# A two-layer decoder trunk on Trainium2: another order of loads, pooling and sums in the first stage

## What is computed

```python
h = rms_norm(x, norm_g[i, 0]) * (1.0 + scale1) + shift1
y = pool_mixer(h)      # layer 0;  layer 1: differential attention
x = x + gate1 * rms_norm(y, norm_g[i, 1])
h = rms_norm(x, norm_g[i, 2]) * (1.0 + scale2) + shift2
y = swiglu(h)          # layer 0;  layer 1: top-2-of-8 experts
x = x + gate2 * rms_norm(y, norm_g[i, 3])
```

## Time and profile before

| | |
|---|---|
| median of three runs | 1278.63 us |
| the profiled execution's own time | 1280.07 us |
| its span | 1278.2 us |
| TensorE busy | 1249.0 us, 98% |
| VectorE, ScalarE, GpSimd busy | 387.3, 214.7, 109.8 us |
| mean granted TensorE clock | 0.991 of full speed |
| moved by DMA | 477.47 MB, mean 374 GB/s |
| first FFN matmul (end of the first stage) | 70.39 us |

### The profile page before, as it was taken

One profiled execution on the slowest core, in us unless ns is written; L12 is line 12 of the kernel. 1 busy time (PEld: TensorE's weight loads), 2 busy tenths in 40 slices (PEclk: granted clock), 3 DMA queues, 4 the chain that ended last, 5 costly groups with the idle time before them and its releaser, 6 DMA issues.

```text
span 1278.2 us, 31266 instructions
## 1 busy us (share of the span) xinstructions
PE 1249.0 (98%) x14625; PEld 779.1 (61%) x14625; DVE 387.3 (30%) x591; ACT 214.7 (17%) x320; POOL 109.8 (9%) x134
## 2 busy tenths in 40 slices
PE   6799999999999999999999999999999999999997
PEld 3589999989774354545455454554545545454555
DVE  1567778979872110101101011010101201011012
ACT  3253333474842000000000000000000000000001
POOL 4220000010030000020010010002001000200100
PEclk9899999999999999999999999999999999999999
DMA  9998998959379999999999999999999999999980
GB/s 371 414 358 295 334 333 305 364 197 395 123 245 420 425 423 425 424 402 424 424 407 424 424 409 411 424 409 404 423 421 396 422 424 412 404 424 415 399 355 36
DMA packets 114055, 477.47 MB, mean 374 GB/s; under 512 B 10944, under 2 KB 37280, under 8 KB 113792
## 3 DMA queue, kind: packets, MB, share of 16 engines
q1 hardware_dynamic: 106112, 457.29, 89.1%
q0 software_dynamic: 7664, 17.87, 4.6%
q10 hardware_dynamic: 144, 0.26, 0.1%
HBM read 465.79 MB, written 11.16 MB: 373 GB/s over the span
## 4 chain that ended last, share of the span: by engine, by line
PE 95%; DVE 2%; ACT 1%; POOL 1%; DMA 1%; issue 1%; SPq 0%; DVEq 0%; ACTq 0%
PE ps L2421 23%; PE ps L2407 23%; PE ps L2396 23%; PE ps L1927 7%; PE ps L1928 7%; PE ps L1929 7%; PE ps L1952 1%; PE ps L2014 1%; PE ps L1911 1%; DMA raw<-w_mod 1%; DVE wlo L1572 1%; PE ps L2205 1%; PE ps L1975 0%; PE ps L2035 0%; PE ps L2350 0%
## 5 line engine op out<-in xcount | busy, mean ns | idle before, releaser
L1799 DVE TENSOR_TENSOR act_in<-act_in,ps 128x1344 f32<-128x1344 f32 x16 | 24.9, 1555 | 527.1 <-PE ps L2407 527.1
L1927 PE MATMUL ps<-thi,whi 128*128 128x256 f32 x480 | 136.0, 283 | 0.8 <-DVE wlo L1421 0.8
L1928 PE MATMUL ps<-tlo,whi 128*128 128x256 f32 x480 | 135.8, 283 | 0.0
L1929 PE MATMUL ps<-thi,wlo 128*128 128x256 f32 x480 | 135.8, 283 | 0.0
L2396 PE MATMUL ps<-raw,turned_in 128*32 128x448 f32 x1296 | 123.7, 539 | 0.0
L2407 PE MATMUL ps<-ring_w,turned_in 128*32 128x448 f32 x1248 | 120.6, 539 | 0.0
L2421 PE MATMUL ps<-ring_w,turned_act 128*32 128x256 f32 x2016 | 117.2, 379 | 0.0
L2421 PE MATMUL ps<-raw,turned_act 128*32 128x256 f32 x2016 | 115.5, 379 | 0.0
L1220 ACT ACTIVATE act_in<-ps 128x1344 f32<-128x1344 f32 x16 | 20.7, 1292 | 548.6 <-PE ps L2396 548.6
L1290 DVE TENSOR_TENSOR wlo<-raw,whi 128x2048 fp32r<-128x2048 f32 x41 | 92.9, 2289 | 32.7 <-ACT whi L901 32.7
L2421 PEld LDWEIGHTS ps<-raw,turned_act 128*32 128x32 f32 x2016 | 82.4, 110 | 33.5 <-issue 3.5
(11 more groups left out here) (324 smaller groups left out, 1332.0 us busy)
## 6 DMA issues: line engine op xcount, KB each, us to landing
raw<-moe_w_gu SPq DMA_DIRECT2D x96, 896.0 KB, 12.9
ring_w<-moe_w_gu SPq DMA_DIRECT2D x96, 896.0 KB, 13.0
raw<-w_mod SPq DMA_DIRECT2D x84, 512.0 KB, 5.7
rows<-moe_w_gu SPq DMA_DIRECT2D x48, 896.0 KB
raw<-moe_w_down SPq DMA_DIRECT2D x48, 896.0 KB, 13.9
ring_w<-moe_w_down SPq DMA_DIRECT2D x48, 896.0 KB, 13.4
raw<-ffn_w_gu SPq DMA_DIRECT2D x44, 512.0 KB, 5.6
rows<-moe_w_down SPq DMA_DIRECT2D x24, 896.0 KB
```

Source lines behind the costliest of these rows:

```text
L1799: dve.tensor_tensor(act_3, act_3, gate_up_ps(1), ALU.mult).then_inc(e_act, 1)
L1927: pe.matmul(out, a_hi, b_hi, start=start, stop=False, skip_group_check=check)
L1928: pe.matmul(out, a_hi, b_lo, start=False, stop=False, skip_group_check=check)
L1929: return pe.matmul(out, a_lo, b_hi, start=False, stop=stop, skip_group_check=check)
```

## The change

Nothing is computed in another way; transfers, matmuls and copies are put in another order, with other banks.

- **Loads.** The tokens are loaded first, ahead of unit 0; the bands follow unit 0. A unit's load now waits until the unit two before it has landed (units 2 to 11).
- **TensorE.** After unit 1 it pools; unit 2, `spread` 1 (banks 2 and 3), unit 3 and the turn of group 1 come behind the pooling, then `m1`, unit 4, and the mix of tile 1. Units 5, 7 and 9 follow that mix. Group 4's columns are turned ahead of the first token turn. Units are called one at a time, in the same order.
- **ScalarE.** The squares of the tokens come first, then the copies of columns and distances, the scalings, and both wide copies ahead of group 1's sum.
- **Banks.** Groups 1 and 3 in bank 1, 0 and 4 in bank 0; `m1` in bank 1, gate1's sum in banks 2 and 3, `keep_clock` in bank 3.
- **Zeros** are written by VectorE at its start, and TensorE waits for them once, at its start.

```diff
@@ -49,7 +49,7 @@
 HEAD_ORDER = (1, 0, 4, 3)
 HEAD = [(1, 0), (1, 1), (1, 2), (1, 3), (0, 0), (0, 1), (2, 0), (0, 2), (2, 1), (0, 3), (2, 2), (2, 3),
         (4, 0), (4, 1), (4, 2), (4, 3), (3, 0), (3, 1), (3, 2), (3, 3)]
-HEAD_BANK = {1: 7, 0: 0, 4: 2, 3: 3}
+HEAD_BANK = {1: 1, 0: 0, 4: 0, 3: 1}
 WIDE = 6
@@ -123,7 +123,7 @@
 ROW_ORDER = [[2, 5], [3, 2, 4, 5]]
-ROW_BANK = [[None, None, 0, None, None, 2], [None, None, 0, 2, 6, 6]]
+ROW_BANK = [[None, None, 2, None, None, 2], [None, None, 0, 2, 6, 6]]
 ROW_GAIN = {2: 1, 4: 2, 5: 3}
@@ -556,8 +556,8 @@
         def _(sp):
             def load(r, rounds, halves):
-                if 3 <= r < RAW + WIDE:
-                    _, landed, n = head_slot(r - 3)
+                if 2 <= r < RAW + WIDE:
+                    _, landed, n = head_slot(r - 2)
                     sp.wait_ge(landed, n)
                 if RAW + WIDE <= r < R_FFN + RAW:
                     u = r - RAW - WIDE if r < 2 * RAW + WIDE else r - RAW
@@ -604,11 +604,11 @@
             sp.dma_start(silu_c[:, :], c.rearrange("a (p k) -> (a p) k", k=KC)).then_inc(c_loaded, 16)
+            sp.dma_start(xs[:, :, :], x[0].rearrange("(t p) d -> p t d", p=P)).then_inc(x_loaded, 16)
             for r, (g, pair) in enumerate(HEAD):
                 load(r, 0, mod_unit(0, g, pair))
-                if r == 1:
+                if r == 0:
                     sp.dma_start(pool_band, pool_in.rearrange("p (g s) -> p g s", g=4)).then_inc(pool_loaded[0], 16)
-                    sp.dma_start(xs[:, :, :], x[0].rearrange("(t p) d -> p t d", p=P)).then_inc(x_loaded, 16)
                 if r == 3:
                     sp.dma_start(poolw, pool_w[0].rearrange("g (c p) e -> p g c e", p=P)).then_inc(pool_loaded[1], 16)
@@ -728,7 +728,6 @@
             pool.memset(bias_row[:, S:S + P], NEG).then_inc(dist_ready, 1)
             pool.memset(minus_half[:, :], -0.5).then_inc(half_ready, 1)
             pool.memset(rows[:, 5, :], 0.0).then_inc(rows_zeroed, 1)
-            pool.memset(zeros[:, :], 0.0).then_inc(zeros_ready, 1)
             pool.wait_ge(rows_zeroed, 2)
             pool.dma_start(rows[0:1, 5, :], b_mod[0:1, 5 * D:6 * D]).then_inc(bmod_loaded[1], 16)
@@ -934,22 +933,20 @@
             act.wait_ge(c_loaded, 16)
             act.activation(silu_c[:, :], silu_c[:, :], ACT.Silu).then_inc(silu_ready, 1)
+            def copy_wide(i, b, dst):
+                act.wait_ge(wide_ps, i + 1)
+                act.copy(dst.rearrange("p (h d) -> p h d", h=2), ps[:, b:b + 2, :]).then_inc(wide_ready, 1)
+            for t in range(T):
+                square_x(0, t)
             act.wait_ge(cols_ps, 1)
...
             act.activation(bias_row[:, 0:S], ps[0:NH, 5, 0:S], ACT.Copy, scale=HD ** 0.5).then_inc(dist_ready, 1)
-            def copy_wide(i, b, dst):
-                act.wait_ge(wide_ps, i + 1)
-                act.copy(dst.rearrange("p (h d) -> p h d", h=2), ps[:, b:b + 2, :]).then_inc(wide_ready, 1)
-            for t in range(T):
-                square_x(0, t)
-            copy_wide(0, 2, rows[:, 6, :])
             for t in range(T):
                 normalize_tile(0, t)
+            copy_wide(0, 2, rows[:, 6, :])
+            copy_wide(1, 2, gain[:, 1, :])
             head_sum(1)
             act.wait_ge(col_ready, 1)
             for b in range(4):
@@ -957,7 +954,6 @@
                 for k in (2 * b, 2 * b + 1):
                     act.activation(pooled_t[:, k, :], ps[:, 4 + b, (k % 2) * S:(k % 2) * S + S], ACT.Copy,
                                    scale=modc[:, 0, k:k + 1]).then_inc(pooled_ready, 1)
-            copy_wide(1, 1, gain[:, 1, :])
             square_mixed(1)
             head_sum(0)
             square_mixed(0)
@@ -1378,6 +1374,7 @@
                 dve.wait_ge(col_step, i + 1)
                 return dve.tensor_tensor(modc[:, 2 * i, :], modc[:, 4, :], cols[:, 6 + i, :], ALU.mult)
+            dve.memset(zeros[:, :], 0.0).then_inc(zeros_ready, 1)
             dve.wait_ge(pool_loaded[0], 16)
             dve.tensor_copy(pool_m[:, :, 0:EDGE], pool_band[:, :, BAND:BAND + EDGE]).then_inc(pool_placed, 1)
             dve.tensor_copy(pool_m[:, :, EDGE:P], pool_band[:, :, EDGE:P]).then_inc(pool_placed, 1)
@@ -1394,7 +1391,7 @@
                 dve.wait_ge(pooled_ready, k + 1)
                 g = k // 2
-                dve.scalar_tensor_tensor(pooled_t[:, k, 0:EDGE], ps[:, 3, g * EDGE:g * EDGE + EDGE], modc[:, 1, k:k + 1],
+                dve.scalar_tensor_tensor(pooled_t[:, k, 0:EDGE], ps[:, 1, g * EDGE:g * EDGE + EDGE], modc[:, 1, k:k + 1],
                                          pooled_t[:, k, 0:EDGE], ALU.mult, ALU.add).then_inc(pooled_done, 1)
             gate_unit(2)
             gate_unit(3)
@@ -1962,35 +1959,14 @@
                                    start=True, stop=True, skip_group_check=True)
                 mm.then_inc(col_ps, 1)
-            pe.wait_ge(silu_ready, 1)
-            head_units(range(0, 2))
-            pe.wait_ge(consts_loaded, 16)
-            pe.wait_ge(mcol_loaded, 64)
-            pe.transpose(ps[:, 6, 0:9 * KC], mcol, ident[0:9 * KC, 0:9 * KC]).then_inc(cols_ps, 1)
-            pe.wait_ge(small_loaded, 32)
-            pe.matmul(ps[0:NH, 5, 0:S], relb, onehot, start=True, stop=True).then_inc(dist_ps, 1)
             def spread(i, b):
...
                 mm.then_inc(wide_ps, 1)
-            pe.wait_ge(scale_loaded, 16)
-            spread(0, 2)
-            head_units(range(2, 4))
-            turn_columns(1)
-            pe.wait_ge(wide_ready, 1)
-            pe.wait_ge(pool_placed, 2)
-            for g in range(4):
-                mm = pe.matmul(ps[:, 3, g * EDGE:g * EDGE + EDGE], ones, pool_band[:, g, 0:EDGE], start=(g == 0), stop=True,
-                               skip_group_check=True)
-            mm.then_inc(m1_ps, 1)
-            pe.wait_ge(dist_ready, 2)
-            pe.wait_ge(col_ready, 1)
-            pe.wait_ge(h_ready, T)
-            for b in range(4):
+            def pooled(b):
                 for t in range(T):
                     for k in (2 * b, 2 * b + 1):
                         c0 = (k % 2) * S
@@ -2003,10 +1979,6 @@
                                            start=False, stop=True, skip_group_check=True)
                 mm.then_inc(pooled_ps, 1)
-            pe.wait_ge(first_gain_loaded, 16)
-            spread(1, 1)
-            head_units((4, 5))
             def mix(t):
                 for g in range(4):
@@ -2016,14 +1988,45 @@
                                        start=(g % 2 == 0 and k == 0), stop=(k == 1), skip_group_check=True)
                 mm.then_inc(mix_ps, 1)
+            pe.wait_ge(zeros_ready, 1)
+            pe.wait_ge(silu_ready, 1)
+            head_units((0,))
+            pe.wait_ge(consts_loaded, 16)
+            pe.wait_ge(mcol_loaded, 64)
+            pe.transpose(ps[:, 6, 0:9 * KC], mcol, ident[0:9 * KC, 0:9 * KC]).then_inc(cols_ps, 1)
+            pe.wait_ge(small_loaded, 32)
+            pe.matmul(ps[0:NH, 5, 0:S], relb, onehot, start=True, stop=True).then_inc(dist_ps, 1)
+            pe.wait_ge(scale_loaded, 16)
+            spread(0, 2)
+            head_units((1,))
+            pe.wait_ge(pool_placed, 2)
+            pe.wait_ge(h_ready, T)
+            pe.wait_ge(cols_ready, 1)
+            pe.wait_ge(dist_ready, 2)
+            for b in range(4):
+                pooled(b)
+            head_units((2,))
+            pe.wait_ge(wide_ready, 1)
+            pe.wait_ge(first_gain_loaded, 16)
+            spread(1, 2)
+            head_units((3,))
+            turn_columns(1)
+            pe.wait_ge(wide_ready, 2)
+            pe.wait_ge(col_ready, 1)
+            for g in range(4):
+                mm = pe.matmul(ps[:, 1, g * EDGE:g * EDGE + EDGE], ones, pool_band[:, g, 0:EDGE], start=(g == 0), stop=True,
+                               skip_group_check=True)
+            mm.then_inc(m1_ps, 1)
+            head_units((4,))
+            pe.wait_ge(pooled_ready, KC)
             pe.wait_ge(scale_folded, 2)
-            pe.wait_ge(pooled_ready, KC)
             mix(MIX_ORDER[0])
-            head_units((7, 9))
+            head_units((5,))
+            head_units((7,))
+            head_units((9,))
             turn_columns(0)
             pe.wait_ge(pooled_done, KC)
             mix(MIX_ORDER[1])
-            pe.wait_ge(wide_ready, 2)
             pe.wait_ge(gate_done, 4)
             row_sum(0, 2)
@@ -2036,16 +2039,21 @@
                     if t:
                         mm.then_inc(ht_ps, 1)
-            head_units(range(12, 16))
+            pe.wait_ge(col_ready, 2)
+            head_units((12,))
+            head_units((13,))
+            head_units((14,))
             pe.wait_ge(gated, T)
+            head_units((15,))
+            turn_columns(4)
             turn(0)
-            turn_columns(4)
-            head_units(range(16, 17))
+            head_units((16,))
             turn(1)
-            head_units(range(17, 20))
+            head_units((17,))
+            head_units((18,))
```

(15 more changed lines are left out.)

## The result

The changed kernel takes 1281.76 us (median of 13 runs, 1281.0 to 1283.02) against 1279.74 us of the kernel before, measured beside it in 13 runs (1278.0 to 1280.9). The ratio is 1.0021, 95% interval 1.0013 to 1.003: about 2 us slower, just clear of no change. The profiled executions stand at 1281.74 us (span 1279.9) and 1280.07 us (span 1278.2), 1.7 us apart. The forecast was 1281.5.

What follows compares the result with a forecast made beforehand. From the first FFN matmul (70.39 us) one engine, TensorE, is the bound, so only that start matters: -0.5 + 0.96 + 2.2 + 0.3 = +2.9 us. Against the median 1278.63 that gave 1281.5, range 1277.8 to 1284.8 us.

Steps and rivals of the forecast that it cites:

- Pooling ahead of the scale: Before the first mix: units 2 and 3 behind the pooling give its gain back; mix at 32.4, not 32.94: -0.5 us.
- Unit 5 behind the mix: Between first mix and turn of the shift columns: three units instead of two, +0.96 us.
- The clock at the mix: At the first mix: PE half idle beforehand, so its clock falls and the mix runs partly cold, +2.2 us.
- Shift, second mix, gates: From the shift columns on: order as before, so the row sum and VectorE residual inherit the delay, some +2.7 us.
- Turn stage: Column turn ahead of token turn: PE waits for head 4's copy, +1.3, offset by the clock; +0.3 us net.
- the clock's return 5.5 us behind the columns: In the turn stage: array returns to full speed 5.5 us after the scale columns end, as before the change.
- Two units in flight: In the loading queue: each load waits for the unit two before; cost 0, bounds 0 and 0.9 us a unit.
- The cover: In the loading queue: the unit still under way covers 2.5 us, against 2.15 us overhead of a 3.4 us transfer.
- the idle share of the DMA: Sign of the rival that the queue runs dry (1283.6 us, chance 0.10): over a tenth idle in 12 to 36 us.
- The rival that the level holds: At the first mix: PE's clock stays 1.00 from 32 to 38 us, +0.7 in all, 1279.3 us; chance 0.22.

Runs made afterwards that it cites:

- run 9: Changed kernel with units 2 and 3 between the second and third pooled group and the second spread behind the pooling, no zeros added; 1282.0 us, ratio 1.0026.
- run 10: Changed kernel with the second spread (four one-row matmuls) and its copy moved behind the first mix and unit 5; 1282.03 us, ratio 1.0028.
- run 5: Changed kernel with 48 matmuls of zeros behind unit 15, ahead of the turn stage; 1279.95 us, ratio 1.0007 to the kernel before.
- Run 4: Changed kernel with unit 5 ahead of the first mix again; 1282.28 us, ratio 1.0017 to the kernel before.
- run 1: Changed kernel with 8 and 16 matmuls of zeros in the pauses ahead of the first mix; 1283.36 us, ratio 1.0026 to the kernel before.
- run 2: Changed kernel with the first token turn ahead of group 4's column turn again; 1281.33 us, ratio 1.0009 to the kernel before.
- run 11: The kernel of run 8 without its matmuls of zeros, except the 24 at the head's end; 1280.28 us, ratio 1.0009 to the kernel before.
- Run 3: Changed kernel with three units in flight again instead of two; 1282.33 us, ratio 1.002 to the kernel before.
- run 8: Changed kernel with units 2 and 3 among the pooling, unit 5 before the mix, later second spread, three units in flight, token turn first, zeros; 1276.76 us, ratio 0.9983.
- run 7: Kernel before with 60 matmuls of zeros ahead of the first token turn; 1277.06 us, ratio 0.9983 to the unedited kernel before.
- run 12: The kernel before, unchanged, profiled once more; own time 1280.38 us, span 1278.6.

## Why the prediction was right

The forecast was +2.9 us on the profiled time and 1281.5 for the median; measured were +1.7 between the profiles and +2.0 between the medians. That 1281.5 comes within 0.3 of 1281.76 is luck: the step was 0.9 smaller than forecast, and the kernel before, measured again, stood at 1279.74 and not at the 1278.63 that I started from. The direction and the largest term are not luck. By its steps:

- **Pooling ahead of the scale, forecast -0.5, measured -1.06** (31.88 against 32.94). The mechanism is as told: the scale's columns are ready at 28.8 (28.9 forecast) because units 2 and 3 and the spread stand behind the pooling, and ScalarE's scalings stand alone. The size was off mostly because eight of them in a row take 3.02 us, not 3.4: the 0.84 of the earlier trace rows is the time from the start of a pair to its end, and in a row the next one starts sooner. Runs 9 and 10 show the mechanism: with unit 3 sooner, the mix starts at 29.3 and 29.6. The size belongs to this execution: in run 5, with the same order, the mix started at 33.34, behind the clock's earlier fall.
- **Unit 5 behind the mix, forecast +0.96, measured +0.94** in the changed kernel's own timeline (38.20 to 41.0 for three units, 36.59 to 38.52 for two). Run 4, with the unit ahead of the mix, won nothing of it in the time; in its profile the unit ran at the lower level, but there the clock had fallen ahead of the edit.
- **The clock at the mix, forecast +2.2, measured +2.67** (6.39 against 3.72, clock 0.50 in 32 to 34). It is the largest term, and the level was the reason, as told. What brings the fall was told too narrowly: the forecast reads it off pauses, but here the clock fell ahead of the pause at the mix, in run 9 without any pause, and in runs 1, 4 and 5 not behind the pause of 1.52 us. The three terms give +2.55, and the edge steps came 2.48 later.
- **Shift, second mix, gates: inherited**, as told. The second mix took 5.41 us in both kernels.
- **Turn stage, forecast +0.3, measured -0.7.** PE did wait for head 4's copy until 60.82, but the clock came back at about the same moment as before, before 66 (0.84 against 0.70 in 64 to 66), though the stage began 2.4 us later. The step that failed is the clock's return 5.5 us behind the columns: these ended at 61.83 and the clock was back near 64.6, 2.8 us behind them. This is the term that was mis-sized, and the main reason that +2.9 came out as +1.8. Its size changes from one execution to the next: in run 2 the clock stayed low until 68 us, in run 11 until 67. I took its value from one execution, with bounds of -0.7 and +3.1; -0.7 was the lower one.
- **Two units in flight, forecast 0, measured 0**, but the queue was thinner than I took it to be: PE waited for unit 15 until 56.32, where it had 52.04, 4.3 us of the slack. The cover was reckoned against 3.4 us, the least of the earlier trace rows, which are of a stretch under traffic and not of an empty queue; their median is 5.2. In 14 to 46 us of the changed kernel a 512 KB transfer into `ring_w` took 4.7 us to land (median of twelve), and 6.8 before. Run 3 shows that nothing of this reached the end. The Trainium skill (DMA: Bandwidth & Descriptors, "Latency and other measured facts") ties the fixed cost to the load on memory; no run here parts a fixed cost from the rest, so that stays open. The sign that I named for it, the idle share of the DMA, would have missed it.

The rival that the level holds fell with the clock of 32 to 34. The Trainium skill (TensorE: Matmul & The Clock Gate, "HAM oscillation") has its rule on pauses, by which it would have held. The trace disagrees: what PE did before the fall was a column turn, edge sums and a part of unit 4, with pauses of 0.49 and 0.63 us.

## What to carry to other kernels

In a stage of short dependent steps, price a stretch of pauses and narrow matmuls on TensorE with what runs behind it at half speed, not with its own length: here pauses of 0.49 and 0.63 us and narrow work stood in front of a mix that took 2.7 us more. Moving wide matmuls forward left narrow ones and waits behind, and in all nine profiles with the pooling first and no zeros ahead of the fall it fell before or under the first mix; filled with zeros, in run 8, it held. So an order and its filling have to be judged together, and the fill belongs where the clock is still up: run 11's order was no quicker than the kernel before without zeros and beat it with them. And take such prices from several executions: where the clock falls and returns differs from one to the next.

## What the runs showed that was not expected

- Zeros count. In run 7 they are the only edit, and the clock stayed at 1.00. In run 5, 48 of them ran at half speed in part (3.62 us), and the clock came back while PE did nothing else; in run 1, 24 came too late to pay.
- The kernel before, unchanged, varies by as much as the whole change is worth: its 104 timed executions lie at 1277.3 to 1278.8 and at 1279.6 to 1281.4 us, and none between. The moment of the clock's return is the likely cause, and not shown (run 12).
- The clock fell in run 9 with no pause on PE, and did not fall behind a pause of 1.52 us in runs 1, 4 and 5.
- Two units of 1 MB in flight moved 363 GB/s, three moved 419, while the busy share of the DMA engines read 0.99 and 1.03.
